# Summing eight groups of expert outputs in PSUM and gathering from the unscaled stream, in a two-layer fp32 trunk on one core

## The reference

```
x = x + mix(rms_norm(x) @ w_in) @ w_out
h = rms_norm(x) * norm_ffn_g
# router: best of 4 groups, then the best 2 of its 8 experts; gates from two softmaxes
x = x + sum over the 2 chosen experts e of gate_e * ((silu(h @ w_gate[e]) * (h @ w_up[e])) @ w_down[e])
```

## Time and profile before

| | |
|---|---|
| median of 3 runs | 1185.41 us (1182.15 to 1186.55) |
| profiled execution, own time | 1184.4 us |
| its span, first to last instruction | 1182.7 us |
| mean granted TensorE clock | 0.888 |
| TensorE matmul busy | 886.5 us, 75% |
| VectorE busy | 506.9 us, 43% |
| ScalarE busy | 171.3 us, 14% |
| DMA, share of 16 engines' span | 90.2% |
| HBM read | 440.30 MB |

### The profile page before, as it was taken

One profiled execution on the slowest core, in us unless ns is written; L12 is line 12 of the kernel. 1 busy time (PEld: TensorE's weight loads), 2 busy tenths in 40 slices (PEclk: granted clock), 3 DMA queues, 4 the chain that ended last, 5 costly groups with the idle time before them and its releaser, 6 DMA issues.

```text
span 1182.7 us, 20427 instructions
## 1 busy us (share of the span) xinstructions
PE 886.5 (75%) x8533; PEld 528.6 (45%) x8533; DVE 506.9 (43%) x1311; ACT 171.3 (14%) x479; POOL 43.1 (4%) x98
## 2 busy tenths in 40 slices
PE   9999997775747575757799999977767575666656
PEld 6577575342424242424465675733424232333234
DVE  2977475332424241424338664743424242323233
ACT  2334211100000000000013341101000000000000
POOL 2001120000000000000000120000000000000000
PEclk9999999887889797878899999988968788888878
DMA  8946579999999999999996274899999999999996
GB/s 276 383 180 245 228 302 425 428 427 427 428 426 430 429 426 430 429 427 426 412 387 268 72 268 185 352 420 424 428 427 428 428 429 427 429 429 426 429 426 289
DMA packets 55853, 442.23 MB, mean 374 GB/s; under 512 B 9440, under 2 KB 12528, under 8 KB 30704
## 3 DMA queue, kind: packets, MB, share of 16 engines
q1 hardware_dynamic: 55792, 441.37, 90.2%
HBM read 440.30 MB, written 1.05 MB: 373 GB/s over the span
## 4 chain that ended last, share of the span: by engine, by line
PE 59%; DMA 27%; DVE 10%; issue 2%; ACT 1%; SPq 1%; DVEq 0%
DMA ring<-in_expert_w_up 25%; PE psum L850 15%; PE psum L884 8%; PE psum L865 8%; PE psum L893 6%; PE psum L968 5%; PE psum L749 5%; PE psum L823 4%; DVE work L1501 2%; DMA maps<-in_expert_w_down 1%; PE psum L985 1%; PE psum L916 1%; DVE work L1507 1%; DVE work L1512 1%; DVE work L1503 1%
## 5 line engine op out<-in xcount | busy, mean ns | idle before, releaser
L850 PE MATMUL psum<-ring,work 128*32 128x256 f32 x3712 | 251.3, 431 | 92.6 <-DMA ring<-in_expert_w_up 92.6
L865 PE MATMUL psum<-ring,work 128*32 128x256 f32 x1664 | 146.2, 511 | 130.6 <-DVE work L1507 126.3
L850 PEld LDWEIGHTS psum<-ring,work 128*32 128x32 f32 x3712 | 139.7, 125 | 205.2 <-issue 153.3
L865 PEld LDWEIGHTS psum<-ring,work 128*32 128x32 f32 x1664 | 62.9, 139 | 202.3 <-DVE work L1507 148.9
L1499 DVE TENSOR_SCALAR work<-work 128x128 f32<-128x128 f32 x62 | 14.2, 229 | 305.5 <-ACT work L1172 305.5
L1512 DVE COPY work<-psum 32x256 f32<-32x256 f32 x124 | 52.6, 424 | 159.7 <-PE psum L865 158.6
L884 PE MATMUL psum<-ring,hT 128*128 128x512 f32 x224 | 98.5, 594 | 1.7 <-ACT work L1195 1.7
L749 PE MATMUL psum<-work,h 128*128 128x128 f32 x512 | 65.4, 289 | 32.9 <-DVE work L1464 26.3
L1176 ACT ACTIVATE work<-psum 32x256 f32<-32x256 f32 x124 | 46.2, 373 | 291.0 <-PE psum L865 290.3
L749 PEld LDWEIGHTS psum<-work,h 128*128 128x128 f32 x512 | 62.2, 202 | 46.2 <-DVE work L1464 36.7
L893 PE MATMUL psum<-hT,ring 128*128 128x256 f32 x320 | 70.7, 380 | 0.0
(11 more groups left out here) (295 smaller groups left out, 781.3 us busy)
## 6 DMA issues: line engine op xcount, KB each, us to landing
ring<-in_expert_w_gate SPq DMA_DIRECT2D x64, 2048.0 KB, 17.7
ring<-in_expert_w_up SPq DMA_DIRECT2D x60, 2048.0 KB, 22.1
ring<-in_expert_w_down SPq DMA_DIRECT2D x52, 2048.0 KB, 21.4
ring<-in_w_in SPq DMA_DIRECT2D x10, 2048.0 KB, 18.4
work<-in_expert_w_down SPq DMA_DIRECT2D x6, 2048.0 KB, 17.1
ring<-in_w_out SPq DMA_DIRECT2D x4, 2048.0 KB, 8.0
ring<-in_w_in SPq DMA_DIRECT2D x8, 512.0 KB, 13.5
maps<-in_expert_w_down SPq DMA_DIRECT2D x2, 2048.0 KB, 8.5
```

The costliest lines, as they stand in the source:

```text
L850: last = T.matmul(bank[GU_BANK[i % 2]][CAP * j:CAP * j + CAP, 0:2 * P], xg[:, k, CAP * i:CAP * i + CAP], gate_up[:, :, k, P * j:P * j + P] ...
L865: last = T.matmul(bank[5][CAP * q:CAP * q + CAP, 0:2 * P], actT[i % 2][:, CAP * j:CAP * j + CAP], down[j][:, 2 * P * q:2 * P * q + 2 * P], ...
```

## The change

- The four scatter matmuls of every group go to the same banks 0 to 3 (`SUM_BANK`). The first group of a layer starts the sum and the others add to it in PSUM. VectorE adds to `x` once a layer, in `last_experts`, and the per-group adds are gone.
- `h` is no longer written. The gather's stationary operand is `x` itself, read with a step of eight elements (32 bytes), and `sel` holds the token's inverse root in place of 1. `sel` is built by four tensor-scalar operations and one add; before it was two tensor-scalar operations and two fused ones.
- The gather goes to banks 4 and 6, the transposes of `gat` to bank 7, the token counts to bank 7, the keep-warm matmuls to bank 0.
- The 8 KB of `h` are now `aside`. The second half of expert 3's down matrix is loaded there while the mixer's end is computed, behind the last rows of expert 0's up matrix. The load into `maps` after expert 1 is gone, and expert 5's gate matrix, which stood behind it, now waits for `gu_ps` of 2, not for `ye_ps` of 2.
- In the last group the wait for `gat_sb` stands ahead of the last expert's up half, because both use bank 7.

```diff
-        FIRST = [(3, IN_ROWS, 5), (2, AHEAD, IN_MAPS), (0, 1, IN_WORK), (4, XTRA, IN_MAPS)]
+        FIRST = [(3, IN_ROWS, 5), (2, AHEAD, IN_MAPS), (0, 1, IN_WORK), (4, XTRA, ASIDE)]
...
                 e.dma_start(u[:, 4:6, :], up[:, 0:2, :]).then_inc(full, 16)
+                e.wait_ge(oa_sq.sem, oa_sq.after(l, 2))
+                half_down(aside[:, :, :, :].rearrange("p j k c -> p j (k c)"), ASIDE, 3, 1)
                 e.wait_ge(op_ps.sem, op_ps.after(l, 4))
...
                 part(ring_full, four[2], 4, 2)
-                e.wait_ge(main.ye_ps.sem, main.ye_ps.after(first, 2))
-                half_down(slot(IN_MAPS).rearrange("p (j n) -> p j n", j=4)[:, 2:4, :], IN_MAPS, 3, 1)
+                e.wait_ge(main.gu_ps.sem, main.gu_ps.after(first, 2))
                 part(ring_full, five[0], 5, 0)
...
-                            last = T.matmul(bank[half][:, k * P:k * P + P], h[:, i, 4 * half + k, :], sel[:, i, :],
+                            rows = x[:, i, :].rearrange("p (c k) -> p k c", k=KT)
+                            last = T.matmul(bank[GU_BANK[half]][:, k * P:k * P + P], rows[:, 4 * half + k, :], sel[:, i, :],
                                             start=(i == 0), stop=(i == TI - 1))
...
-                    T.matmul(bank[(6, 7, 0, 1)[n]][:, :], gatT[:, i * P:i * P + P], ye[:, half * 512:half * 512 + 512],
-                             start=True, stop=True).then_inc(S.scat_ps.sem, 1)
+                    T.matmul(bank[SUM_BANK[n]][:, :], gatT[:, i * P:i * P + P], ye[:, half * 512:half * 512 + 512],
+                             start=(order is OVERLAPPED), stop=False).then_inc(S.scat_ps.sem, 1)
...
-                    e.wait_ge(rstd_mixed.sem, rstd_mixed.after(l, i + 1))
-                    A(h[:, i, :, :], x[:, i, :].rearrange("p (c k) -> p k c", k=KT), ACT.Copy, scale=rstd[:, i:i + 1]).then_inc(h_ok.sem, 1)
...
-                for n in range(4):
-                    e.wait_ge(S.scat_ps.sem, S.scat_ps.after(turn, n + 1))
-                    xs = x[:, n // 2, n % 2 * 512:n % 2 * 512 + 512]
-                    TT(xs, bank[(6, 7, 0, 1)[n]][:, :], xs, ALU.add).then_inc(S.x_added.sem, 1)
                 c.end()
...
+                other = gtmp_first if prepare else gtmp
                 for i in range(TI):
-                    TS(sel[:, i, :], iota[:, :], codes[:, i:i + 1], None, ALU.is_equal).then_inc(c.step(), 1)
-                e.wait_ge(c.sem, c.last())
+                    TS(sel[:, i, :], iota[:, :], codes[:, i:i + 1], rstd[:, i:i + 1], ALU.is_equal, ALU.mult).then_inc(c.step(), 1)
                 for i in range(TI):
-                    last = STT(sel[:, i, :], iota[:, :], codes[:, TI + i:TI + i + 1], sel[:, i, :], ALU.is_equal, ALU.add)
-                    if i < TI - 1:
-                        last.then_inc(c.step(), 1)
-                last.then_inc(S.sel_ok.sem, 1)
+                    TS(other[:, i, :], iota[:, :], codes[:, TI + i:TI + i + 1], rstd[:, i:i + 1], ALU.is_equal, ALU.mult).then_inc(c.step(), 1)
+                e.wait_ge(c.sem, c.last())
+                TT(sel, sel, other, ALU.add).then_inc(S.sel_ok.sem, 1)
+                e.wait_ge(S.sel_ok.sem, S.sel_ok.after(turn, 1))
```

## The result

The changed kernel takes 1190.72 us (median of 5 runs, 1189.58 to 1191.63), the kernel before 1184.15 us beside it. The ratio is 1.0054, with a 95% interval from 1.0036 to 1.0073: some 6.4 us slower, where 4.5 us less were forecast. The profiled execution took 1191.07 us with a span of 1189.3.

What follows compares the result with a forecast made beforehand. The prediction took the weight stream to bound the flat stretches at 428 GB/s, and mixer and router the uneven ones. Its terms, -4.90 + 0.90 + 0.40 - 0.95 = -4.55 us, gave 1180.9 us, range 1177 to 1185.8.

Steps and rivals of the forecast that it cites:

- Term 3: First gather of each layer: loads stepping by 32 bytes cost 0.2 us a gather, +0.4 us in all; upper bound 1.6 each.
- The rule that stands beside the term: Gather's loads from SBUF: each new 16-byte line costs extra, fp32 steps up to 4 are free; 3.2 us over both layers.
- The second rival: Gather: stepped loads take twice as long without overlap and set TensorE's pace, 8.6 us per first gather, 1197.8 us; chance 0.04.
- In the others the wait for weights takes it up.: Gathers after each layer's first group: the stepped loads' extra time hides under TensorE's wait for weights and costs nothing.
- Term 1: Half of expert 3's down matrix: 1 MB per layer leaves the flat stretch for a DMA hole, -4.90 us over two layers.
- Term 2: Building sel ahead of each layer's first gather: ready 0.45 us later, moving the flat stretch twice, +0.9 us.
- Term 4: Layer 1's queue, dry from 795 to 801: the issue at 794.83 comes at least 4 us earlier, gaining 0.95 us.
- Edits costed at nothing: Adds to x and hand-over, write of h, banks, expert 5's gate issue and last group's gat_sb wait: no time change.

Runs made afterwards that it cites:

- e4: The changed kernel with each group's 16 gather matmuls reading x at steps of 1, 2, 4 and 8 elements, four each; ran once, 1183.22 us.
- e6: The changed kernel with the first group of each layer gathering from packed x, the other seven with the step; 1181.01 us, ratio 0.9981 to the kernel before.
- e7: The changed kernel with all gathers packed and the half of expert 3's down matrix loaded into maps again; 1182.76 us, ratio 0.9992 to the kernel before.
- e1: The changed kernel with all gathers reading x packed instead of with the step of eight; 1178.54 us, ratio 0.9957 to the kernel before.
- e3: The changed kernel with h and its gather, the old selection and the half matrix in maps restored; 1182.22 us, ratio 0.9991 to the kernel before.

## Why the prediction was wrong

It was wrong in one term of its sum, the price of the stepped gather, and in what it let that term touch.

- **Term 3, the stepped gather.** Forecast 0.2 us a gather, with 1.6 as the upper bound; measured 3.8 to 4.1. This is the step that failed. The nearest row was a transpose of the same view of `x`, and its load (191 ns, spacing 0.121) was no price for a matmul's: that load takes 336 ns and comes every 0.242 us. Transposes came every 0.11 us with loads of 141 as with loads of 191 ns, so the step could hide in them. The spacing of 0.121 was no steady price either: eight such transposes at 594.80 in the changed kernel took 0.97 us, 0.111 apart. The bound was wrong too. It added the transposes' 50 ns to the old spacing, but the step adds 144 ns to a load, and as the overlap stays what it was, nearly all of it shows: (0.242 - 0.114) x 32 = 4.1 us. The rule that stands beside the term, of the Trainium skill, SBUF — State Buffer, section "Door 1: The DMA port swizzle", spoke for the costlier side, and a step of 8 is costly; its border, free up to a step of 4, did not hold here (330 ns, e4). The second rival had the loads set the pace, as they do, and put it at 8.6 us a gather, with a chance of 0.04: its load was to take twice as long and takes 1.75 times, and its overlap was to vanish and did not.
- **"In the others the wait for weights takes it up."** Mostly. The 14 later gathers cost 2.8 us in all by the medians (e6), and 6.8 in its profiled execution, through dry spots that no row of before shows. The term belonged in the sum with a price of its own, 3.85 us more ahead of an issue in each hand-over.
- **Term 1, the megabyte.** Right in mechanism and size: 4.90 us forecast, 4.2 measured between e7 and e1.
- **Term 2, the selection.** Right: from expert 2's gate matrix to the first paced load e1 takes 0.44 and 0.38 us more than the kernel before, where 0.45 was forecast. As for `sel` itself, it is built in 160.88 + 0.43 - 159.73 = 1.58 us in the changed kernel, as worked out. The rows:

```profile
159.73 0.60 DVE L1458 TENSOR_SCALAR work<-iota,small 128x128 f32<-128x128 f32 x2
160.24 0.60 DVE L1460 TENSOR_SCALAR work<-iota,small 128x128 f32<-128x128 f32 x2
160.88 0.43 DVE L1462 TENSOR_TENSOR work<-work 128x256 f32<-128x256 f32 x1
```

- **Term 4, the dry queue.** The queue can be kept full there (e3: 423 GB/s), but the 0.95 us were not seen as time. In e3 the stretch is as long as before, and in e1 it is 2.49 us shorter (1147.77 - 749.97 against 400.29), which the megabyte's 2.45 explain alone. The issue that was to come at least 4 us earlier came 41.41 us behind the first paced load before (794.83 - 753.42), 34.22 in e1 and 40.93 in the changed kernel. The slow second gather, 7.67 us, took 3.9 of that gain away, and TensorE at the lower clock ahead of it some 2.8 us (the scatter of 5.41). The spot at 801 loses more than the old one did.
- **Edits costed at nothing.** With packed gathers the sum without term 3 is -4.95 us, 0.42%, and e1 measured 0.43%, with an interval of 0.28 to 0.58%. By that interval the adds, the write of `h` and the banks, with term 4, are within some 2 us of what was forecast. The close match is partly luck: in the profiles e1's span is 5.3 us shorter, of which 4.74 lie in the flat stretches, 1.7 are the clock at the start of layer 1, which was in no term, and 0.64 are lost in the tail, without a cause that the runs show.

The clock at the start of layer 1 (-1.7 us in the profiled execution) was in no term. Without it the profiled loss would have been larger.

## What to carry to other kernels

Before an operand is read from another layout, ask for the price of that very kind of instruction in that layout; here a transpose's load was no price for a matmul's. The load of a stationary fp32 operand was as good as free at a step of 2, took 1.4 times as long at 3 and 1.7 times from 4 on, and a chain of such loads grew by nearly all of that. Where transfers are the bound, as here, an engine's delay is paid in full ahead of the first paced transfer and at a small and varying part of its size inside the stretch, in the moments when the queue runs dry: so put the packed copy where the first use is, and let the memory that it frees carry bytes only after that.

## What the runs showed of the hardware that was not expected

- Loads of 128x128 fp32 for a matmul: 192, 196, 261, 330, 318 and 337 ns at steps of 1, 2, 3, 4, 6 and 8 elements. For a transpose: 140, 206 and 192 ns at 1, 2 and 8.
- Packed loads of 192 ns come every 0.11 us, stepped ones of 336 ns every 0.24: the load grows by 144 ns and the spacing by some 130, because two neighbouring loads overlap by 80 to 100 ns at any step.
- Sums held open in four PSUM banks over the groups of a layer, with the transposes, gathers and up matmuls of other banks between them, made neither scatters nor packed gathers slower: a scatter took 3.67 us at full clock before and after, a gather 3.81 to 3.84 us before and 3.73 to 3.84 in e1.
- The scatters took 3.67 us at full clock and 5.3 to 5.9 us where the mean granted clock in them was 0.62 to 0.69: three of the changed kernel's fourteen in the profiled execution, none of e1's.
